# Expert token lists made ahead of the loop, and expert outputs kept in three gathered accumulators, in a hybrid attention and mixture-of-experts layer

## What is computed

```python
def moe(t, ...):                      # t: 576 x 1024, after the first layer norm
    scores = sigmoid(t @ w_router)    # 64 experts; 4 of 8 groups, then the best 8 experts
    gates = one_hot(top_e) * scores / sum(scores of the 8) * 2.5
    for wg, wu, wd, g in experts:     # 1024x256, 1024x256, 256x1024, f32
        h = silu(t @ wg) * (t @ wu)
        acc = acc + (h @ wd) * g[:, None]
    shared = (silu(t @ w_gate_s) * (t @ w_up_s)) @ w_down_s
    return acc + shared
x2 = layer_norm(ALPHA * x1 + moe(x1))
```

## Time and profile before

| | us |
|---|---|
| median of 3 runs | 1369.98 (1368.73 to 1371.9) |
| the profiled execution | 1368.96 |
| its span in the trace | 1367.1 |
| first to last `hh` (one per expert) | 609.4 to 1321.2 |
| TensorE / DVE / ACT / POOL busy | 1237.0 / 775.5 / 543.4 / 406.6 |
| share of the chain that ended last | TensorE 79%, DVE 10%, issue 5% |

### The profile page before, as it was taken

One profiled execution on the slowest core, in us unless ns is written; L12 is line 12 of the kernel. 1 busy time (PEld: TensorE's weight loads), 2 busy tenths in 40 slices (PEclk: granted clock), 3 DMA queues, 4 the chain that ended last, 5 costly groups with the idle time before them and its releaser, 6 DMA issues.

```text
span 1367.1 us, 18465 instructions
## 1 busy us (share of the span) xinstructions
PE 1237.0 (90%) x6931; PEld 972.6 (71%) x6931; DVE 775.5 (57%) x1095; ACT 543.4 (40%) x722; POOL 406.6 (30%) x385
## 2 busy tenths in 40 slices
PE   6999788899999989879999999999999999999980
PEld 6999566899999986346666666666666666666750
DVE  3124794631234345258776766666666666667735
ACT  4213573522214121134544444444444444445522
POOL 2000342210110114334433333433444433333223
PEclk9999997799999988989999999999999999999995
DMA  9941301022325038158999999999999999999944
GB/s 287 216 108 33 102 1 70 17 92 63 95 90 193 6 133 337 50 201 302 369 356 342 344 339 344 340 339 342 346 350 344 342 335 340 338 344 348 356 97 155
DMA packets 91616, 314.74 MB, mean 230 GB/s; under 512 B 15698, under 2 KB 48644, under 8 KB 66324
## 3 DMA queue, kind: packets, MB, share of 16 engines
q1 hardware_dynamic: 72160, 260.25, 50.2%
q0 software_dynamic: 18688, 53.37, 19.0%
q10 hardware_dynamic: 708, 0.28, 0.1%
HBM read 284.30 MB, written 45.22 MB: 241 GB/s over the span
## 4 chain that ended last, share of the span: by engine, by line
PE 79%; DVE 10%; issue 5%; DMA 2%; ACT 2%; POOL 2%; DVEq 0%; ACTq 0%; POOLq 0%
PE bank L1928 27%; PE bank L1948 16%; PE bank L1665 10%; PE bank L1664 10%; PE bank L1823 4%; DVE onehot L1504 4%; PE bank L1891 3%; PE bank L1679 3%; PE bank L1853 2%; DVE L L1259 1%; PE bank L1844 1%; DVE mx L1265 1%; DMA y_rows<-ysb,idx_u 1%; PE bank L1870 1%; DVE ysb L1544 1%
## 5 line engine op out<-in xcount | busy, mean ns | idle before, releaser
L1528 DVE TENSOR_TENSOR wgu_lo<-wgu,wgu_hi 128x4096 fp32r<-128x4096 f32 x64 | 282.6, 4416 | 2.7 <-ACT wgu_hi L1128 2.7
L807 POOL TENSOR_TENSOR spare<-spare 128x1 f32<-128x1 f32 x128 | 119.8, 936 | 445.0 <-DMA y_rows<-ysb,idx_u 408.9
L1948 PE MATMUL bank<-wd,hT 128*128 128x512 f32 x512 | 230.1, 592 | 0.9 <-DVE hT L1538 0.9
L1128 ACT ACTIVATE wgu_hi<-wgu 128x4096 fp32r<-128x4096 f32 x63 | 227.4, 3609 | 0.0
L1928 PE MATMUL bank<-wgu_hi,xgT 128*128 128x512 f32 x512 | 205.2, 401 | 2.6
L1928 PE MATMUL bank<-wgu_hi,xgT_lo 128*128 128x512 f32 x512 | 200.0, 391 | 0.0
L1928 PE MATMUL bank<-wgu_lo,xgT 128*128 128x512 f32 x512 | 199.9, 390 | 0.0
L1132 ACT ACTIVATE silu<-bank 128x256 f32<-128x256 f32 x64 | 24.5, 383 | 367.3 <-PE bank L1928 367.3
L1948 PEld LDWEIGHTS bank<-wd,hT 128*128 128x128 f32 x512 | 96.7, 189 | 98.0 <-issue 92.0
L1544 DVE COPY ysb<-bank 128x512 f32<-128x512 f32 x64 | 44.3, 692 | 163.2 <-PE bank L1948 163.2
L1928 PEld LDWEIGHTS bank<-wgu_hi,xgT 128*128 128x128 f32 x512 | 96.3, 188 | 23.4 <-issue 0.5
(11 more groups left out here) (287 smaller groups left out, 2431.6 us busy)
## 6 DMA issues: line engine op xcount, KB each, us to landing
wgu<-in_w_gate_e_dram SPq DMA_DIRECT2D x64, 1024.0 KB, 9.2
wgu<-in_w_up_e_dram SPq DMA_DIRECT2D x64, 1024.0 KB, 13.8
wd<-in_w_down_e_dram SPq DMA_DIRECT2D x64, 1024.0 KB, 7.8
raw<-in_w_in_dram SPq DMA_DIRECT2D x16, 1024.0 KB, 5.9
raw<-in_w_proj_a_dram SPq DMA_DIRECT2D x4, 1024.0 KB, 5.1
raw<-in_w_out_dram SPq DMA_DIRECT2D x4, 1024.0 KB, 5.2
x_lo_kept<-xT_lo SPq DMA_DIRECT2D x1, 2304.0 KB, 10.7
x_lo_back<-x_lo_kept SPq DMA_DIRECT2D x1, 2304.0 KB, 8.4
```

Source lines behind the costliest of these rows:

```text
L807: pool.tensor_tensor(spare[:, i:i + 1], spare[:, 0:1], spare[:, 0:1], ALU.mult).then_inc(s, 1)
L1128: act.activation(wgu_hi[u % 2][:], wgu[u % WSLOTS][:], ACT.Copy).then_inc(hi_by_act, 1)
L1528: v.tensor_tensor(wgu_lo[u % WSLOTS][:], w_[:], wgu_hi[u % 2][:].bitcast(F32), ALU.subtract).then_inc(lo_by_dve, 1)
L1948: last = mm(bank[3 + h][:, :], hT[:, u % 2, j, :], wd[slot][:, j, h * 512:(h + 1) * 512], start=j == 0, stop=j == FE // P - 1)
```

## The change

1. **Lists ahead.** `places` runs in an earlier round of the shared expert. DVE computes for every token and each of its eight experts a slot number, `slot_u`. POOL scatters the token number to these slots of a DRAM table `owner`, which SP filled with out-of-range indices early on: 5 tiles x 8 indirect DMAs of 4 bytes per partition. POOL then reads the table back as `idx_all`, one index column per expert. `onehot`, `R`, `gate_idx`, `token_list` and `sent` are gone. The gates are stored as 64 more columns of `x1_rows`, and arrive with the gathered rows (`xg`, 1088 wide).
2. **Accumulators.** `y_rows` becomes three DRAM tensors; the second and third are zeroed by POOL. For expert e, POOL gathers the rows of tensor `acc[e]` (e modulo 3; in the last four experts 0 and 1 in turn) into `yg`, DVE adds the product from PSUM in two halves (`y_add`), and POOL scatters them back without accumulation. Out-of-range indices are skipped.
3. **Order.** POOL issues in each step y gather, x gather, scatter. All loops are written out, none is a Fori.
4. **Halves and engines.** The copy to `wgu_hi` and the subtraction to `wgu_lo` are two instructions each. The evacuation of `hT` goes from DVE to ACT. In the shared expert DVE multiplies and adds straight from PSUM, where ACT and POOL did.
5. **End.** SP reads three tensors back, and DVE adds the other two to the first in each tile.

```diff
-UNROLL = 8
-IDX_AHEAD = 4
+NACC = 3
+FAR_SLOT = 65536
...
+    acc = [e % NACC if e < E - 4 else e % 2 for e in range(E)]
+    turn = [acc[:e + 1].count(acc[e]) for e in range(E)]
...
 @block.gpsimd
-            pool.dma_start(y_rows[TOK:TOK + P, :], sgln[:].rearrange("p a n -> p (a n)")).then_inc(y_zeroed, 16)
+            for i in range(1, NACC):
+                for t, (a, w) in enumerate(TILES):
+                    pool.dma_start(y_rows[i][a:a + w, :], sgln[0:w].rearrange("p a n -> p (a n)")).then_inc(y_zeroed, 16)
...
+            pool.wait_ge(owner_cleared, 16 * NT)
+            pool.wait_ge(route_dve, 1)
+            for t, (a, w) in enumerate(TILES):
+                for r in range(8):
+                    pool.indirect_dma_start(out=owner, out_offset=bass.IndirectOffsetOnAxis(slot_u[0:w, t, r:r + 1], 0),
+                                            in_=token_id[0:w, t:t + 1], in_offset=None).then_inc(owner_written, 16)
+            pool.wait_ge(owner_written, 16 * NT * 8)
+            pool.dma_start(idx_all[:, :], owner.rearrange("(t p e) a -> t p (e a)", t=NT, p=P)[0]).then_inc(idx_landed, 16)
...
+            for e in range(XGSLOTS - 1):
+                gather_x(e, xg_in[e], idx_all[:, e:e + 1])
...
+            for e in range(E):
+                if e >= NACC:
+                    pool.wait_ge(y_put[acc[e]], 16 * (turn[e] - 1))
+                gather_y(acc[e], idx_all[:, e:e + 1])
+                n = e + XGSLOTS - 1
+                if n < E:
+                    if e >= 1:
+                        pool.wait_ge(h_by_dve, e)
+                        pool.wait_ge(ex_xt, e)
+                    gather_x(n % XGSLOTS, xg_in[n % XGSLOTS], idx_all[:, n:n + 1])
                 if e >= 1:
-                    scatter(e - 1, e - 1, e == 1)
+                    pool.wait_ge(y_by_dve, 2 * e)
+                    scatter_y(acc[e - 1], idx_all[:, e - 1:e])
...
 @block.scalar
-                act.activation(wgu_hi[u % 2][:], wgu[u % WSLOTS][:], ACT.Copy).then_inc(hi_by_act, 1)
+                for h in range(2):
+                    act.activation(wgu_hi[u % 2][:, h], wgu[u % WSLOTS][:, h], ACT.Copy).then_inc(hi_by_act, 1)
...
 @block.vector
+            v.tensor_scalar(slot_u[:], top8[:], -1.0, float(FAR_SLOT), ALU.mult, ALU.add).then_inc(route_dve, 1)
...
+            def y_add(e, i):
                 v.wait_ge(ex_dn, e + 1)
-                if free:
-                    v.wait_ge(y_added, (e - 1) * 16)
-                v.tensor_copy(ysb[:, u % 2, 512:1024], bank[4][:, :]).then_inc(y_by_dve, 1)
+                for h in range(2):
+                    c = slice(h * 512, (h + 1) * 512)
+                    v.tensor_tensor(yg[i][:, c], yg[i][:, c], bank[3 + h][:, :], ALU.add).then_inc(y_by_dve, 1)
...
+            for e in range(E):
+                if e + 1 < E:
+                    xt_evac(e + 1, e + 1)
+                    weights_lo(e + 1, e + 1)
+                hidden(e, e, slice(D + e, D + e + 1))
+                if e >= 1:
+                    v.wait_ge(y_got[acc[e - 1]], 16 * turn[e - 1])
+                    y_add(e - 1, acc[e - 1])
...
             for t in range(NT):
-                v.wait_ge(y_back[t], 16)
+                v.wait_ge(y_back[t], 32)
+                then(v.tensor_tensor(x1[0:w, t, :], x1[0:w, t, :], y_other[0][0:w, t, :], ALU.add))
+                if NACC > 2:
+                    v.wait_ge(y_third, 16 * NT)
+                    then(v.tensor_tensor(x1[0:w, t, :], x1[0:w, t, :], y_other[1][0:w, t, :], ALU.add))
...
 @block.tensor
-                if t == NT - 3:
+                if t == 1:
                     places()
...
+            rows_t(0, 0, 16)
+            for e in range(E):
+                if e + 1 < E:
+                    rows_t(e + 1, e + 1, 16 * ((e + 1) // XGSLOTS + 1))
+                gate_up(e, e)
+                if e >= 1:
+                    down(e - 1, e - 1, (e - 1) // WSLOTS + 1)
+                hidden_t(e, e)
```

More of the change, by code:

```diff
@@ L240, in hybrid_layer @@
     selm = in_j("selm", [P, NT, E])
-    R = in_j("R", [P, NT, E, 6], BF16)
     chosen = in_j("chosen", [P, NT, E], BF16)
-    posm = in_j("posm", [P, NT, E])
-    onehot = in_j("onehot", [P, 4, NT, P], BF16)
+    gates = in_j("gates", [P, NT, E])
+    slot_u = in_j("slot_u", [P, NT, 8], U32)
     hh = in_j("hh", [P, 2, FE])
@@ L592, in _ @@
                 if n == RAW:
+                    sp.wait_ge(pool_consts, N_CONST)
+                    for t in range(NT):
+                        sp.dma_start(owner.rearrange("(t p e) a -> t p (e a)", t=NT, p=P)[t], idx_all[:, :]).then_inc(owner_cleared, 16)
                     load(tm_bias[:, 0:P], A["b_in"][0:1, KE:VE].to_broadcast([P, P]))
@@ L683, in _ @@
             sp.wait_ge(most_dve, 1)
             sp.wait_ge(ex_dn, E)
+            for i in range(NACC):
+                sp.wait_ge(y_put[i], 16 * uses[i])
             most_r = sp.value_load(most[0:1, 0:1], min_val=0, max_val=TOK)
             with sp.If(most_r > P):
+                if NACC > 2:
+                    sp.wait_ge(y_third, 16 * NT)
                 for tile in range(1, NT):
+                    if tile > 1:
+                        sp.wait_ge(y_put[0], 16 * (uses[0] + E * (tile - 1)))
+                    sp.dma_start(idx_all[:, :], rows[tile]).then_inc(idx_again, 16)
@@ L726, in _ @@
             const(pool.memset(mv[:], 1.0))
-            const(pool.memset(spare[:], 1.0))
             n_set = k[0]
@@ L869, in _ @@
+            pool.wait_ge(y_by_dve, 2 * E)
+            scatter_y(acc[E - 1], idx_all[:, E - 1:E])
+            for i in range(NACC):
+                pool.wait_ge(y_put[i], 16 * uses[i])
             most_r = pool.value_load(most[0:1, 0:1], min_val=0, max_val=TOK)
             with pool.If(most_r > P):
+                pool.memset(spare[:], 1.0).then_inc(pool_step, 1)
                 for tile in range(1, NT):
@@ L1140, in _ @@
             ex_xt_evac(0, 0)
[L1141 to L1142 removed]
+            act.wait_ge(sy_dve, 2 * NT)
+            act.wait_ge(x1_written, 16 * NT)
             weights_hi(1, 1)
[L1144 to L1157 removed]
@@ L1159, in _ @@
-            for e in range(UNROLL):
-                step(e, e, 0, first=e == 0, free=e >= 3)
-            with act.Fori(1, E // UNROLL - 1) as i:
-                for u in range(UNROLL):
-                    step(i * UNROLL + u, u, i)
-            for e in range(E - UNROLL, E):
-                step(e, e % UNROLL, E // UNROLL - 1, last=e == E - 1, ahead=e + 2 < E)
-            ex_y(E - 1, E - 1)
-            act.wait_ge(y_added, 16 * E)
+            for e in range(E):
+                if e + 1 < E:
+                    ex_xt_evac(e + 1, e + 1)
+                if e >= 1:
+                    ex_ht_evac(e - 1, e - 1)
+                    act.wait_ge(h_by_dve, e)
+                ex_silu(e)
+                if e + 2 < E:
+                    weights_hi(e + 2, (e + 2) // WSLOTS + 1)
@@ L1169, in _ @@
+            ex_ht_evac(E - 1, E - 1)
+            for i in range(NACC):
+                act.wait_ge(y_put[i], 16 * uses[i])
             most_r = act.value_load(most[0:1, 0:1], min_val=0, max_val=TOK)
@@ L1578, in _ @@
-            for e in range(UNROLL):
-                step(e, e, first=e == 0, wait=e + IDX_AHEAD >= UNROLL, free=e >= 3)
-            with v.Fori(1, E // UNROLL - 1) as i:
-                for u in range(UNROLL):
-                    step(i * UNROLL + u, u)
-            for e in range(E - UNROLL, E):
-                step(e, e % UNROLL, ahead=e + IDX_AHEAD < E, last=e == E - 1)
-            ht_evac(E - 1, E - 1)
-            y_evac(E - 1, E - 1)
-            v.wait_ge(y_added, 16 * E)
+            sh_sum(4)
@@ L1589, in _ @@
+            for i in range(NACC):
+                v.wait_ge(y_put[i], 16 * uses[i])
             most_r = v.value_load(most[0:1, 0:1], min_val=0, max_val=TOK)
```

466 lines of the change are left out of this document (176 added, 290 removed).

## The result

The changed kernel takes 1408.0 us (median of 4 runs, 1405.9 to 1410.1) against 1369.7 for the kernel before (1368.7 to 1371.9): ratio 1.0277, 95% interval 1.0257 to 1.0298. It is slower by 38 us. The prediction was 1323, faster, with a range to 1356.

The account below looks back on a forecast made before the run. The prediction took a chain of waits between PE and DVE, with no DMA link, to bound the expert loop. Terms of -80.2, +17.6 and +16.7 sum to -45.9 us, giving 1323 us, 8 in 10 from 1304 to 1356.

Parts of the forecast that it names:

- Term 1: Expert loop: without list work PE sets the step, 10.04 us where it was 11.57; saving 80.2 us.
- Does DMA supply 10.04?: Expert loop: weights 7.73 us and plain rows 2.2 at 407 GB/s, in sum 9.95 us a step, just enough.
- upper end of 12.2: Expert loop: DMA time a step if plain rows move at q0's mixed 203 GB/s; kept only for the range.
- The share of q0: Expert loop: the row queue's part of the DMA engines' time, forecast near 20% though its bytes rise; 35.0% before.
- The list-free steps: Last, straight-line expert steps of the kernel before: 10.04 us each without a list, taken as the new loop's step.
- Latency of the new gather: Expert loop: y's gather is issued early enough, costing nothing unless landings pass 16 us.
- Term 2: Before the loop: x gathers wait for 40 small scatters and a read back, +14.6 us, and a slower clock, +3.
- Term 3: End of the kernel: faster last scatter -4, adding accumulators +12.8, more reads +1.3, DVE meeting POOL +6.6; sum +16.7 us.
- DMA paces by bytes: Expert loop: 361 GB/s is a ceiling, so 4.05 MB need 11.2 us a step; +73 us, 1396; chance 8%.
- POOL holds DVE: Expert loop: three indirect issues a step collide with `wgu_lo`, 0.5 us over; +31 us, 1354; chance 8%.
- Change doesn't do what it says: Expert loop: steps stay near 10.8 to 11.5 us; chance 1%.

Follow-up runs that it names:

- Kernel 16: Changed kernel with a loop moving weights only, rows gathered and scattered just for the first few experts: 1313.0 us.
- kernel 11: Changed kernel with list entries dealt differently over the partitions and, on POOL, the x gather ahead of the y gather and its wait: 1374.8 us.
- kernel 2: Changed kernel loading only half of each expert's down weights, that half used twice: 1343.1 us.
- kernel 3: Changed kernel with 8 instead of 24 matmuls in the gate/up round: 1393.7 us.
- kernel 17: Changed kernel with a loop moving weights only and 8 instead of 24 gate/up matmuls: 1193.5 us.
- kernel 1: Changed kernel with POOL issuing the x gather before the y gather and its wait for a scatter: 1396.2 us.
- kernel 9: Changed kernel with list entry d*16+h*8+r read back to partition h*64+d*8+r, spreading the rows over the engines: 1398.9 us.
- kernel 18: As kernel 10, but experts add in turn into two arrays, each scatter waiting for the one two experts back: 1363.2 us.
- kernel 10: As kernel 4, with the list entries dealt over the partitions as in kernel 9: 1343.2 us, ratio 0.982 to the kernel before.
- kernel 4: Changed kernel without y gathers: POOL scatters with an add into one array, each after the landing of the one before: 1378.2 us.

## Why the prediction was wrong, point by point

**Term 1's step of 10.04 as PE's own: right.** Kernel 16 has 628.5 for the 631.6 of the sum. The first steps of the changed kernel have it too.

**Term 1, "Does DMA supply 10.04?": wrong, and this is the whole miss.** It took the low end, 9.95 us, from 407 GB/s for weights and rows alike. The runs showed 11.1 us a step, at 365 GB/s, with rows spread and issued early (kernel 11), and 11.6 at 349 as the kernel stood. Leaving out half of the down weights brought it to 10.4 (kernel 2); leaving out two thirds of the gate/up work brought only 0.2 us (kernel 3). Three things were wrong in the step.
- *The rate.* 421 GB/s in the earlier trace rows is a stretch of 5 us. Over 300 us weights alone come to 394 at full share (kernel 17), at which 4.05 MB need 10.3 us, already over 10.04; with rows among them it was 11.1. The upper end of 12.2 in the prediction should have weighed more.
- *The mean in place of where the rows stand.* The share of q0 fell as forecast, to 21.7%. But its rows stood on half of the engines, which no share of a loop shows; the spread and x first together gave 35 us of the loop.
- *The list-free steps.* "The same loads, copies and matmuls run in both" does not hold for the steps 1281.94 to 1291.98 of the kernel before. The last gate and up loads were issued at 1285.4 and 1285.9, the last down load at 1294.9, and the DMA share is 0.49 in 1301 to 1310: the steps drew on a stock. For PE's price they are a fair measure, for the supply none.

**"Latency of the new gather ... I cost it at nothing": right for that gather, wrong beside it.** y's gather landed in 15.2 us, inside the 16 that the prediction allowed, and DVE did not wait for it in 800 to 1250. What came late was the x gather, 16.6, since on POOL it stands behind y's wait for a scatter. That path the prediction had not counted: 13.8 us (kernel 1), 24.7 with the rows spread (11 against 9).

**Term 2: mechanism right, size 4 us off.** First row transposes at 609.37 (forecast 611.7):

```profile
545.70 1.10 POOL L823 DMA_INDIRECT owner<-token_id,slot_u  x1 [48.53 <-DVE slot_u L1487]
...
599.32 0.91 POOL L823 DMA_INDIRECT owner<-token_id,slot_u  x1 [0.30 <-issue]
...
604.84 1.05 POOL L830 DMA_INDIRECT xg<-x_rows,idx_all  x1 [2.10 <-DMA idx_all<-owner]
```

The 40 issues take 53.6 us from first to last start, forecast 52 and 4 for DVE; a few were held, up to 3.06 us, the rest went at 1.27. The first `hh` came at +13.4 and not +17.6.

**Term 3: right, 16.7 against 18.7.** Three DVE sums take 3.25 us instead of 1.24 beside a POOL row, 2.0 more each for the forecast 2.2. The arrays are what costs: from last `hh` to the end three of them take 64.6 us, two 53.0 (kernel 18), one 46.1 (kernel 10).

**The rivals.** The outcome was the third, *DMA paces by bytes*, given 8%: step 11.2 and 1396, measured 11.6 and 1408. Against it I had put the 421 GB/s and that an accumulate reads uncounted bytes. The second fits: in kernel 4, 800 to 1200, q0 moved 21.84 MB in 22.4% of the engines' time, in the changed kernel 31.93 MB in 22.0%. That second rate is 363 GB/s at full share; if kernel 4's x rows (35 times 0.31 MB) went at it, its added rows went at some 180, so an added row costs an engine twice a plain one. So by this estimate three plain rows cost an engine what one gathered and one added did. What the change gained on the engines it gained by dropping the empty rows, and not by the accumulators. The Trainium skill, DMA: Bandwidth & Descriptors, Specifications, gives some 358 GB/s as a core's share of HBM, and I set it aside for the 421. Its number, 1403, came within 5 us. That is luck in part: 365 and 386 GB/s were held here, so 358 is not the limit of this loop. *POOL holds DVE* did not pace anything: DVE waits for PE. *Change doesn't do what it says*: in a sense true, since lists left the loop and the step stayed.

What stays open: why nearly full engines move 365 GB/s with rows and 386 without, when short stretches reach 420 to 450; how fast weights alone could go; whether a better deal of the rows than that of kernel 9 gains more; and how the ring of scatters and the engines share the gain of kernel 10.

## What to carry to other kernels

Before costing a loop at its compute step, divide its bytes by a rate that a long stretch has held, and do not take steps that live on a stock as a sign that the loads keep up. Where rows are gathered or scattered through a list with empty entries, look at one such DMA alone: here a share near 0.5 with work waiting meant that half of the engines carried it. Dealing the entries out and reordering the queue were worth 10 and 14 us of the loop alone and 35 together, so try both. Where each transfer waits for the landing of the one before, compare the landing with the step. When a resource is full, moving an issue forward may only decide who is late.
